# Gate projection tiles beside stick breaking and attention: weights loaded earlier, blocks dealt over other places

## The chip, the cores and the metric

The kernel runs on one core of a Trainium2 chip. The metric is the device time in microseconds of one execution; lower is better. Engines in the text: PE is TensorE (matmuls), DVE is VectorE, ACT is ScalarE, SP is the queue that issues the DMAs.

## What is computed

Two blocks of two layers each on 512 tokens of width 1024, in fp32. The second block's layer, cut to what matters here:

```python
def _layer(x, ...):
    h = _rmsnorm(x, norm_g)
    p = _split_columns(h @ w_in)
    y_a = _dsa_attention(q_a, k_a, v_a, qi, ki, p['idx_w'])   # index scores choose the keys
    y_b = _fox_attention(...)
    y_c = _stick_breaking_attention(sb_q, sb_k, sb_v)
    y_d = _nsa_attention(...)
    y_e = _memory_attention(...)
    ys = jnp.stack([y_a * silu(dsa_z), ..., y_e * silu(mem_z)], axis=2)
    merge = jax.nn.sigmoid(p['merge'].reshape(B, S, 5, D_MODEL))
    merged = jnp.sum(merge * jnp.einsum('bsnc,ncd->bsnd', ys, w_branch), axis=2)
    return x + merged @ w_out

def stick_breaking(q, k, v):
    z = q @ k.T * scale
    log_keep = where(strict, log_sigmoid(-z), 0)
    later = cumsum(log_keep, reverse=True) - log_keep
    a = where(strict, exp(log_sigmoid(z) + later), 0)
    return a @ v

# index scores: relu(qi_h @ ki.T) for 4 heads, weighted by idx_w and summed, causal
```

`merge` is a projection of `h` onto 5 x 1024 columns, 40 tiles of 128 columns.

## The kernel before

**Precision and gate blocks.** A weight tile (1024 x 128) is split in two fp32r parts: ACT casts the high part (`extra_high`, L1224), DVE subtracts to get the low part (`extra_low`, L1249). A tile is 8 blocks of 128 input channels; `block_passes` (L224 to L226) runs three matmuls for each block: high x high, high x low, low x high, 512 columns each.

**Extra.** 24 of the 40 gate tiles of a layer (3 of the 5 branches for each of 8 output tiles) are not computed in merge but "beside" other phases, while PE would wait there. The class `Extra` holds how many tiles, and a list of named slots with a number of blocks each. On PE, `extra_products(..., name)` runs the next blocks of that slot; at a tile's first block it waits for `split` (the low part of that tile) and for `evacuated` (the single PSUM bank is free again). On ACT, `extra_evacuations(name)` evicts all tiles that end up to that slot, and `extra_highs(name)` casts the tile two further on. On DVE, `extra_lows(name)` writes its low part. `slots_of` computes from the list which tiles are done by which name. SP loads the raw weights (`extra_load`) and writes evicted tiles to DRAM (`g_spill`, L1187), from where merge reads them.

**Order of the phases in a layer of block 2.** `project2` (34 projection tiles and small work beside them), `stick_breaking` (with 5 gate tiles), `attention` (with 19 gate tiles), `merge`. Each phase is a block with its own semaphores that ends with a barrier over all engines.

**Stick breaking** (L2908). On PE: logits of head 0 (four matmuls j = 0 to 3, L2959, in banks 0, 1, 2 and part of 1), slot "lead", then for each head h: index products of query block h+1 (four index heads, L2948), slot ("first", h), logits of head h+1, cumulative sums of head h (L2975, L2978, banks 4 to 6), slot h, product with the values (L2986). ACT: both first casts, then for each head the evacuation of the logits (L3002, L3003), Exp and Ln (L3005, L3007) in `logarithm`; in the loop the evictions of gates, relu of the index products (L3015), `logarithm(h+1)`, casts, and the Exp that gives the weights (L3027). DVE: low parts, softplus (L3038, L3043, L3047), index scores (`weigh`), the subtraction of the sums (L3076, then `less`), softplus of the next head, then `extra_lows`, then the output (L3084). The slots are 8 for lead, 2 before the logits of heads 1 to 3, then 6, 6, 6 and 8: 40 blocks. Index products use three banks, so the fourth waits for the first relu. The loads of the first four gate tiles are issued at the start of the phase, into `x`, whose space the projections still use for other weights up to their 32nd tile.

**Attention** (L2697). 12 pairs of heads x 4 query blocks make 48 steps; the loop runs s = -2 to 50. In step s PE runs the transposes of step s-1, the logits of s+2 (L2746), slot ("early", s), the values of s-2 (L2776), slot s. DVE masks (L2851), normalises (L2870), and up to step 31 ranks the index scores (L2881, L2887). Each slot has 2 blocks for s >= 0, so 4 a step; 19 tiles are 152 blocks and end with step 37. After all spills have landed SP issues the first loads for merge (`load_merge`, L1179).

Of the kernel before, what the change touches and what calls it, by code (L numbers as in the profile page):

```python
# [13 lines left out]
F32 = mybir.dt.float32  # L14
# [3 lines left out]
ACT = mybir.ActivationFunctionType  # L18
# [1156 lines left out]


def load_merge(sp, core, n, slot_w, width, src):

    sp.dma_start(core.ring[:, n * slot_w:n * slot_w + width], src).then_inc(core.landed[2][n], 16)  # L1179
# [1106 lines left out]

def project2(nc, core, units, b, p, gain, tmp, u_high, u_low, loads, landed, last_gain=None):

# [28 lines left out]
    with phase(nc, *LANDED, "projected", "evacuated", "scaled", "rounded", "split", *NORM, *OPENING, "params", "x_normed", "x_spilled",  # L2317
# [14 lines left out]
        def _(sp):  # L2332
# [22 lines left out]
            for n in range(RING, count):  # L2355
# [27 lines left out]
                if n == 30:  # L2383
                    sp.wait_ge(sems["mv_mm"], 1)
                    sp.dma_start(w1, b["w1_dram"]).then_inc(sems["w1_landed"], 16)
            sp.wait_ge(sems["params"], 16 * len(loads))
            sp.wait_ge(sems["index_copied"], 16)
# [520 lines left out]
def stick_breaking(nc, core, b, p, e):  # L2908
# [12 lines left out]

    cum = [(4, 0), (5, 0), (6, 0), (6, 256)]
    rel, score = b["rel"], b["score"]
# [10 lines left out]
    with phase(nc, *EXTRA, "rel_mm", "rel_out", "weighted", "z_mm", "z_out", "logged", "soft", "cum_mm", "less", "weights", "pv_mm", "y_out", "own", "own_act") as (block, sems):  # L2934
# [5 lines left out]
        def _(pe):  # L2940
            def index_products(i):

                for h in range(4):
                    if h < 3:
                        pe.wait_ge(sems["z_out"], 4 * (i - 1) + (1, 4, 3)[h])
                    else:
                        pe.wait_ge(sems["rel_out"], 4 * (i - 1) + 1)
                    pe.matmul(banks[h % 3][:, 0:(i + 1) * P], qi[32 * h:32 * h + 32, i * P:(i + 1) * P],  # L2948
                              ki[32 * h:32 * h + 32, 0:(i + 1) * P], start=True, stop=True).then_inc(sems["rel_mm"], 1)

            def logits(h):
                m, lo = h // 2, 64 * (h % 2)
                q, k = p[lo:lo + 64, tl["sb_q"] + m, :], p[lo:lo + 64, tl["sb_k"] + m, :]
                for j in range(4):
                    if h and j < 3:
                        pe.wait_ge(sems["rel_out"], 4 * (h - 1) + (4, 2, 3)[j])
                    if j == 3:
                        pe.wait_ge(sems["z_out"], 4 * h + 2)
                    pe.matmul(z_bank(j), k[:, j * P:(j + 1) * P], q[:, j * P:], start=True, stop=True)\  # L2959
                        .then_inc(sems["z_mm"], 1)  # L2960
# [3 lines left out]
            for h in range(4):  # L2964
                m, lo = h // 2, 64 * (h % 2)
                if h < 3:
                    index_products(h + 1)
                    extra_products(pe, sems, core, e, ("first", h))
                    logits(h + 1)
                pe.wait_ge(sems["soft"], h + 1)  # L2970
                if h:
# [19 lines left out]
        def _(act):  # L2991
# [5 lines left out]
            def logarithm(h):  # L2997
                if h >= 2:
                    act.wait_ge(sems["pv_mm"], h - 1)
                for j in range(4):  # L3000
                    act.wait_ge(sems["z_mm"], 4 * h + j + 1)
                    own(act.mul(span(zs, h, j), z_bank(j), SCALE))  # L3002
                    own(act.activation(span(soft, h, j), z_bank(j), ACT.Abs, scale=SCALE))  # L3003
                    own.tell(sems["z_out"])
                own(act.activation(whole(soft, h), whole(soft, h), ACT.Exp, scale=-1.0))  # L3005
                own.settle()
                act.activation(whole(soft, h), whole(soft, h), ACT.Ln, bias=core.ones[:, 0:1]).then_inc(sems["logged"], 1)  # L3007

            def relu(i):
                for h in range(4):  # L3010
                    n = 4 * (i - 1) + h
                    act.wait_ge(sems["rel_mm"], n + 1)
                    if i > 1:
                        act.wait_ge(sems["weighted"], n - 3)
                    act.activation(rel[:, h, 0:(i + 1) * P], banks[h % 3][:, 0:(i + 1) * P], ACT.Relu).then_inc(sems["rel_out"], 1)  # L3015

            extra_high(act, sems, core, e, 0)
            extra_high(act, sems, core, e, 1)
            logarithm(0)
# [11 lines left out]
        def _(dve):  # L3031
# [33 lines left out]

            own(dve.tensor_copy(score(0), causal(0)))
            extra_low(dve, sems, core, e, 0)
            extra_low(dve, sems, core, e, 1)
            softplus(0)
            for h in range(4):  # L3070
# [8 lines left out]
                if h < 3:  # L3079
# [5 lines left out]
                                  ALU.mult).then_inc(sems["y_out"], 1)  # L3085
            dve.wait_ge(sems["y_out"], 4)


# [15 lines left out]
def block2_layer(nc, core, layer, w, con, tables):  # L3104

    with ExitStack() as outer:
# [18 lines left out]
        b["f_abs"], b["f_log"] = buf(inner, "f_abs", [4, 4]), buf(inner, "f_log", [4, 4])  # L3125
        with split_weights(nc, core), nc.sbuf_tensor(f"norm_tmp3{layer}", [P, 4, T], F32) as tmp:
            loads = ((core.small[:, 0:NSMALL2], w["small2"][layer]), (tables[:, :, :], core.t_spill))
            if layer == 0:
                loads += ((con[:, :], w["con2"]),)
            project2(nc, core, lambda n: w["in2"][layer * IN2_TILES + n], b, p,  # L3130
                     core.par[:, PAR2["norm"]:PAR2["norm"] + KD] if layer else core.both_gains[:, :], tmp, u_high, u_low,
                     loads, core.landed[0], None if layer else core.gains[:, 0:KD])

# [3 lines left out]
        def stored_gate(t):  # L3137
            return gates(t // N_STORED * N_BR2 + N_BR2 - N_STORED + t % N_STORED)

        x_flat = core.x[:, :, :].rearrange("p a t -> p (a t)")  # L3140
        beside_stick = 5
        with ExitStack() as stack:
            b["cum"], b["stats"] = buf(stack, "cum", [2, T]), buf(stack, "stats", [3, 6])
            with ExitStack() as scratch:
# [13 lines left out]
                with nc.sbuf_tensor(f"rel{layer}", [P, 4, T], F32) as b["rel"], nc.sbuf_tensor(f"stick_low{layer}", [P, 2, KD * P], F32R) as core.wl:  # L3158
                    stick_breaking(nc, core, b, p, Extra(
                        stored_gate, 0, beside_stick, [("lead", 8), *((slot, n) for h in range(4) for slot, n in ((("first", h), 2 if h < 3 else 0),  # L3160
                                                                                                  (h, 6 if h < 3 else 8)))],
                        core.banks[3:4], [p[:, tl[n], :] for n in ("ckv", "kc_vc")]))
                core.wl = extra_low
# [40 lines left out]
                for m in range(2):  # L3204
                    pairs.append(pair("dsa", m, b["dsa_k"][:, m, :], head(b["dsa_v"], m), lambda h, i: b["score"](i)))
                attention(nc, core, b, pairs, forgotten, Extra(
                    stored_gate, beside_stick, KD * N_STORED - beside_stick,
                    [(slot, 2 if n >= 0 else 0) for n in range(-2, 4 * len(pairs) + 3) for slot in (("early", n), n)],
                    core.banks[7:8], [core.ring[:, n * T:(n + 1) * T] for n in range(2)]), gates)
# [56 lines left out]
def program(nc, w, positions, out):  # L3266
# [6 lines left out]
    with ExitStack() as stack:  # L3273
# [5 lines left out]
        core.count = 0  # L3279
        core.landed = [[stack.enter_context(nc.semaphore(f"{side}_{name}")) for name in LANDED] for side in ("one", "other", "third")]  # L3280
        core.last_spill = stack.enter_context(nc.semaphore("last_spill"))
        core.early = [stack.enter_context(nc.semaphore(f"early_gate{n}")) for n in range(2)]
# [84 lines left out]
```

## Time and profile before

| | us |
|---|---|
| median of 3 runs | 3474.04 (3471.01 to 3476.75) |
| profiled execution, its own time | 3477.62 |
| its span, first to last instruction | 3475.8 |
| granted TensorE clock, mean | 0.978 |

In the rows below, times are microseconds from the span's start. A row of the timeline has the start, the duration, engine, line, operation, output<-input, shapes and count; in brackets the idle time before it and what ended it. PEld is the weight load, which overlaps PE. A busy PE is not PE at its peak, since ends of matmuls are modelled.

### The profile page before, as it was taken

The page shows a single profiled execution, that of the slowest core. Times are in us where ns is not written, and L with a number is a line of the kernel's source. Part 1 is how long each engine was busy: PE and PEld are TensorE (multiplying, and loading weights), DVE is VectorE, ACT ScalarE, POOL GpSimd, SP SyncE. Part 2 cuts the span into 40 slices and gives each one's busy share as a digit, 9 for nine tenths or more (in the row PEclk, how much of TensorE's full clock was granted, in tenths as well). Part 3 has the DMA queues.
Part 4 walks back from the last instruction along what each step waited for, and adds up shares of the span by engine and source line. Part 5 has one row for each costly group of instructions (what it writes and reads, how often), then busy time and mean ns, then how long its engine had stood idle before and what let it go on. Part 6 is the DMA issues. An engine that isn't in the chain of part 4 may idle for free. (4 is left out here: it accounts for less than half of the span.)

```text
span 3475.8 us, 53876 instructions
## 1 busy us (share of the span) xinstructions
PE 3336.0 (96%) x21860; PEld 2610.6 (75%) x21860; DVE 1894.1 (54%) x3265; ACT 1434.2 (41%) x2357; POOL 58.5 (2%) x44
## 2 busy tenths in 40 slices
PE   8998999999999998999999999899899999999898
PEld 6776688788877876887888778566587787566686
DVE  6645634677556446446774452367555631476555
ACT  6423523444255224334443333545533343555532
POOL 0110000000000100000000000000000000000000
PEclk9999999999999999999999999899999999999999
DMA  4324232223232232422223252122152432121341
GB/s 157 95 67 169 97 107 81 103 97 104 100 124 94 76 98 111 155 100 85 97 93 110 102 173 97 40 83 82 35 191 94 152 117 104 47 78 58 127 140 67
DMA packets 106533, 356.86 MB, mean 103 GB/s; under 512 B 12544, under 2 KB 12928, under 8 KB 103488
## 3 DMA queue, kind: packets, MB, share of 16 engines
q1 hardware_dynamic: 106304, 353.67, 30.0%
q8 instruction: 160, 2.62, 0.3%
q14 instruction: 69, 0.57, 0.1%
HBM read 308.93 MB, written 38.80 MB: 100 GB/s over the span
## 5 line engine op out<-in xcount | busy, mean ns | idle before, releaser
L224 PE MATMUL banks<-h_high,weights_high 128*128 128x512 f32 x2464 | 993.8, 403 | 40.6 <-DVE weights_low L245 22.0
L225 PE MATMUL banks<-h_low,weights_high 128*128 128x512 f32 x2464 | 969.9, 394 | 0.0
L226 PE MATMUL banks<-h_high,weights_low 128*128 128x512 f32 x2464 | 969.1, 393 | 0.0
L224 PEld LDWEIGHTS banks<-h_high,weights_high 128*128 128x128 f32 x2464 | 466.8, 189 | 154.0 <-DVE weights_low L245 22.9
L226 PEld LDWEIGHTS banks<-h_high,weights_low 128*128 128x128 f32 x2464 | 466.6, 189 | 102.5
L225 PEld LDWEIGHTS banks<-h_low,weights_high 128*128 128x128 f32 x2464 | 467.3, 190 | 97.6 <-issue 3.3
L217 DVE TENSOR_TENSOR weights_low<-ring,weights_high 128x1024 fp32r<-128x1024 f32 x134 | 167.2, 1247 | 301.4 <-ACT weights_high L212 300.6
L1673 ACT CAST weights_high<-ring 128x1024 fp32r<-128x1024 f32 (+2 forms) x124 | 140.7, 1134 | 457.4 <-PE banks L226 457.2
L1721 DVE TENSOR_TENSOR weights_low<-ring,weights_high 128x1024 fp32r<-128x1024 f32 (+2 forms) x124 | 164.6, 1328 | 294.1 <-ACT weights_high L1673 293.9
L212 ACT CAST weights_high<-ring 128x1024 fp32r<-128x1024 f32 x134 | 140.4, 1048 | 363.9 <-PE banks L226 358.1
L1849 ACT CAST weights_high<-ring 128x1024 fp32r<-128x1024 f32 (+1 forms) x116 | 132.6, 1143 | 334.3 <-PE banks L226 334.3
L1896 DVE TENSOR_TENSOR weights_low<-ring,weights_high 128x1024 fp32r<-128x1024 f32 (+1 forms) x116 | 154.9, 1336 | 93.6 <-ACT weights_high L1849 93.3
L224 PE MATMUL banks<-h_high,extra_high 128*128 128x512 f32 x384 | 169.2, 441 | 1.2 <-ACT ring L1234 1.2
L225 PE MATMUL banks<-h_low,extra_high 128*128 128x512 f32 x384 | 152.7, 398 | 0.0
L224 PE MATMUL banks<-y_high,weights_high 128*128 128x512 f32 x352 | 136.9, 389 | 0.0
L225 PE MATMUL banks<-y_low,weights_high 128*128 128x512 f32 x352 | 136.9, 389 | 0.0
L226 PE MATMUL banks<-y_high,weights_low 128*128 128x512 f32 x352 | 136.9, 389 | 0.0
L224 PE MATMUL banks<-ffn_high,weights_high 128*128 128x512 f32 x352 | 136.9, 389 | 0.0
L225 PE MATMUL banks<-ffn_low,weights_high 128*128 128x512 f32 x352 | 136.9, 389 | 0.0
L226 PE MATMUL banks<-ffn_high,weights_low 128*128 128x512 f32 x352 | 136.9, 389 | 0.0
L226 PE MATMUL banks<-h_high,extra_low 128*128 128x512 f32 x304 | 120.4, 396 | 0.0
L224 PEld LDWEIGHTS banks<-h_high,extra_high 128*128 128x128 f32 x384 | 72.8, 190 | 47.2 <-issue 36.2
(454 smaller groups left out, 5049.5 us busy)
## 6 DMA issues: line engine op xcount, KB each, us to landing
ring<-in_in SPq DMA_DIRECT2D x136, 512.0 KB, 3.8
ring<-in_up SPq DMA_DIRECT2D x88, 512.0 KB, 3.2
ring<-in_gates SPq DMA_DIRECT2D x68, 512.0 KB, 3.6
x<-in_gates SPq DMA_DIRECT2D x60, 512.0 KB, 4.0
ring<-in_down SPq DMA_DIRECT2D x32, 704.0 KB, 4.1
ring<-in_out SPq DMA_DIRECT2D x32, 512.0 KB, 3.3
ring<-in_branch SPq DMA_DIRECT2D x16, 768.0 KB, 4.4
stored<-g_spill SPq DMA_DIRECT2D x16, 768.0 KB, 4.5
```

The costliest lines, as they stand in the source:

```text
L212: act.copy(core.wh[:, half, 0:width], slot(core, s[0], s[1])[:, 0:width]).then_inc(sems["rounded"], 1)
L217: dve.tensor_tensor(core.wl[:, half, 0:width], slot(core, s[0], s[1])[:, 0:width], core.wh[:, half, 0:width].bitcast(F32), ALU.subtract).t ...
L224: pe.matmul(bank, core.wh[:, half, w], high, start=start, stop=False)
L225: pe.matmul(bank, core.wh[:, half, w], low, start=False, stop=False)
L226: return pe.matmul(bank, core.wl[:, half, w], high, start=False, stop=stop)
L1673: act.copy(core.wh[:, n % 2, 0:width(n)], place(n)).then_inc(sems["rounded"], 1)
L1721: dve.tensor_tensor(core.wl[:, n % 2, 0:width(n)], place(n), core.wh[:, n % 2, 0:width(n)].bitcast(F32), ALU.subtract).then_inc(sems["spli ...
L1849: act.copy(core.wh[:, n % 2, 0:width(n)], place(n)).then_inc(sems["rounded"], 1)
L1896: dve.tensor_tensor(core.wl[:, n % 2, 0:width(n)], place(n), core.wh[:, n % 2, 0:width(n)].bitcast(F32), ALU.subtract).then_inc(sems["spli ...
```

## The change

In stick breaking there are now 6 gate tiles and in attention 18. The first two tiles' weights are loaded by SP in `project2` (at its tile 30, behind the load of `w1`) into columns 4096 to 6144 of the ring, each with its own semaphore; ACT waits for that instead of a load of its own phase. Two gate blocks are put into head 0's logits before the fourth matmul, and 3, 3 and 2 into those of heads 1 to 3 at the same place, in place of 2 each ahead of the logits. The slots after the sums have 7, 7, 8, 8 blocks. ACT casts the second tile after head 0's logits have been evacuated, not before. The fourth index product gets a bank of its own (6, shared with the sums); index products wait for all evacuated logits of the head before and for `less`; logits j waits for the relu of its own bank; the sums wait for all four relus. DVE copies the first score row after the first two low parts have been written. In attention the slots have 2 and 2 blocks up to step 15, 2 and 1 up to step 31, 1 and 1 after that.

```diff
+def early_stick(core, t):
+    return core.ring[:, (RING + t) * KD * P:(RING + t + 1) * KD * P]
...
@@ project2, SP
                 if n == 30:
                     sp.wait_ge(sems["mv_mm"], 1)
                     sp.dma_start(w1, b["w1_dram"]).then_inc(sems["w1_landed"], 16)
+                    for t in range(2):
+                        sp.dma_start(early_stick(core, t), first_gates(t)).then_inc(core.early_stick[t], 16)
...
@@ stick_breaking
-    cum = [(4, 0), (5, 0), (6, 0), (6, 256)]
+    cum, rel_banks = [(4, 0), (5, 0), (6, 0), (6, 256)], (0, 1, 2, 6)
...
             def index_products(i):
+                pe.wait_ge(sems["z_out"], 4 * i)
+                if i > 1:
+                    pe.wait_ge(sems["less"], i - 1)
                 for h in range(4):
-                    if h < 3:
-                        pe.wait_ge(sems["z_out"], 4 * (i - 1) + (1, 4, 3)[h])
-                    else:
-                        pe.wait_ge(sems["rel_out"], 4 * (i - 1) + 1)
-                    pe.matmul(banks[h % 3][:, 0:(i + 1) * P], ...)
+                    pe.matmul(banks[rel_banks[h]][:, 0:(i + 1) * P], ...)
...
                 for j in range(4):
                     if h and j < 3:
-                        pe.wait_ge(sems["rel_out"], 4 * (h - 1) + (4, 2, 3)[j])
+                        pe.wait_ge(sems["rel_out"], 4 * (h - 1) + j + 1)
                     if j == 3:
+                        extra_products(pe, sems, core, e, ("first", h - 1))
                         pe.wait_ge(sems["z_out"], 4 * h + 2)
...
                 if h < 3:
                     index_products(h + 1)
-                    extra_products(pe, sems, core, e, ("first", h))
                     logits(h + 1)
+                    pe.wait_ge(sems["rel_out"], 4 * (h + 1))
                 pe.wait_ge(sems["soft"], h + 1)
...
@@ stick_breaking, ACT
                     own.tell(sems["z_out"])
+                if h == 0:
+                    extra_high(act, sems, core, e, 1)
                 own(act.activation(whole(soft, h), whole(soft, h), ACT.Exp, scale=-1.0))
...
             extra_high(act, sems, core, e, 0)
-            extra_high(act, sems, core, e, 1)
             logarithm(0)
...
@@ stick_breaking, DVE
-            own(dve.tensor_copy(score(0), causal(0)))
             extra_low(dve, sems, core, e, 0)
             extra_low(dve, sems, core, e, 1)
+            own.settle()
+            dve.wait_ge(sems["split"], 2)
+            own(dve.tensor_copy(score(0), causal(0)))
             softplus(0)
...
+def beside_attention(steps):
+    slots = []
+    for s in range(-2, steps + 3):
+        early, late = (0, 0) if s < 0 else (2, 2) if s < 16 else (2, 1) if s < 32 else (1, 1)
+        slots += [(("early", s), early), (s, late)]
+    return slots
...
@@ block2_layer
-        beside_stick = 5
+        beside_stick = 6
...
-                        stored_gate, 0, beside_stick, [("lead", 8), *((slot, n) for h in range(4) for slot, n in ((("first", h), 2 if h < 3 else 0),
-                                                                                                  (h, 6 if h < 3 else 8)))],
-                        core.banks[3:4], [p[:, tl[n], :] for n in ("ckv", "kc_vc")]))
+                        stored_gate, 0, beside_stick, [(("first", -1), 2), ("lead", 8), *((slot, n) for h in range(4) for slot, n in (
+                            (("first", h), (3, 3, 2, 0)[h]), (h, (7, 7, 8, 8)[h])))],
+                        core.banks[3:4], [p[:, tl[n], :] for n in ("ckv", "kc_vc")],
+                        [(early_stick(core, t), core.early_stick[t], 16 * (layer + 1)) for t in range(2)]))
...
-                    [(slot, 2 if n >= 0 else 0) for n in range(-2, 4 * len(pairs) + 3) for slot in (("early", n), n)],
+                    beside_attention(4 * len(pairs)),
```

## Rows read from the trace of the kernel before

**Rows 1.** The page's first part: busy time, share of the span, instructions.

```profile
PE 3336.0 (96%) x21860; PEld 2610.6 (75%) x21860; DVE 1894.1 (54%) x3265; ACT 1434.2 (41%) x2357; POOL 58.5 (2%) x44
```

**Rows 2.** Busy time by stretch; stretch, its length, busy by engine, clock, DMA.

```profile
core 0: us, PE busy (x) PEld busy (x) DVE busy (x) ACT busy (x) POOL busy (x), PEclk, DMA share, GB/s
2190.90:2282.90 92.00, 78.96 (x288) 49.67 (x288) 37.42 (x77) 52.27 (x75) 0.00 (x0) 0.89 0.12 43
2282.90:2481.80 198.90, 197.53 (x1140) 135.70 (x1141) 136.01 (x508) 107.13 (x309) 0.00 (x0) 1.00 0.24 75
2361.00:2442.60 81.60, 81.39 (x486) 56.02 (x484) 58.87 (x209) 43.20 (x121) 0.00 (x0) 1.00 0.23 72
2481.80:2515.50 33.70, 24.48 (x197) 15.81 (x195) 16.29 (x75) 22.46 (x69) 0.00 (x0) 0.90 0.11 40
2938.10:3031.10 93.00, 78.76 (x288) 49.72 (x289) 37.42 (x77) 52.31 (x75) 0.00 (x0) 0.89 0.12 43
```

**Rows 3.** PE's waits in layer 0's stick breaking: total, times, longest.

```profile
PE banks L2959 <- ACTq L143: 8.8, 4, 5.3
PE banks L2948 <- ACT rel L3015: 1.7, 3, 0.7
PE banks L2986 <- ACT ring L3027: 1.0, 1, 1.0
```

**Rows 4.** Timeline of the start of layer 0's stick breaking, ACT.

```profile
2194.28 1.04 ACT L1224 CAST extra_high<-x 128x1024 fp32r<-128x1024 f32 x1 [4.15 <-DMA x<-in_gates]
...
2196.58 0.59 ACT L3002 ACTIVATE ring<-banks 128x512 f32<-128x512 f32 x1
...
2203.99 1.37 ACT L3007 ACTIVATE ring<-ring,ones 128x1280 f32<-128x1280 f32 x1
```

**Rows 5.** Timeline from the end of head 0's cumulative sums.

```profile
2218.28 0.48 PE L224 MATMUL banks<-h_high,extra_high 128*128 128x512 f32 x1
...
2218.56 1.68 DVE L3076 SCALAR_TENSOR_TENSOR ring<-banks,ring 128x512 f32<-128x512 f32 x4 [7.08 <-PE banks L2975]
...
2220.39 1.49 DVE L3038 SCALAR_TENSOR_TENSOR ring<-ring 128x1280 f32<-128x1280 f32 x1
...
2221.92 0.90 DVE L3043 TENSOR_TENSOR ring<-ring,con_sb 128x128 f32<-128x128 f32 x4
...
2223.52 0.57 ACT L1234 COPY others<-banks 128x512 f32<-128x512 f32 x1
...
2223.90 1.22 DVE L1249 TENSOR_TENSOR stick_low<-x,extra_high 128x1024 fp32r<-128x1024 f32 x1
```

**Rows 6.** Timeline, PE: the first passes of two gate blocks in succession.

```profile
2203.20 0.39 PE L224 MATMUL banks<-h_high,extra_high 128*128 128x512 f32 x1
...
2203.90 0.39 PE L224 MATMUL banks<-h_high,extra_high 128*128 128x512 f32 x1
```

**Rows 7.** Timeline near the end of the projections: issues on SP, a cast.

```profile
2147.55 7.88 SPq L2357 DMA_DIRECT2D ring<-in_in  x3
...
2163.98 1.05 ACT L212 CAST weights_high<-ring 128x1024 fp32r<-128x1024 f32 x1 [3.11 <-PE banks L226]
```

**Rows 8.** Busy time by stretch, columns as in rows 2: clock 0.50.

```profile
2198.50:2202.60 4.10, 3.86 (x9) 2.98 (x10) 0.00 (x0) 3.72 (x7) 0.00 (x0) 0.50 0.20 80
...
2254.10:2260.90 6.80, 6.70 (x13) 4.05 (x14) 0.00 (x0) 6.37 (x10) 0.00 (x0) 0.50 0.00 0
...
2510.10:2513.50 3.40, 3.40 (x21) 2.73 (x19) 0.00 (x0) 1.44 (x4) 0.00 (x0) 0.50 0.02 5
```

**Rows 9.** PE's waits in attention's steps 38 to 50: total, times, longest.

```profile
PE banks L2762 <- DVE probs L2870: 7.9, 3, 3.5
```

**Rows 10.** Timeline: last spill, merge's loads, its first cast; then their landing.

```profile
2482.65 0.32 SPq L1187 DMA_DIRECT2D g_spill<-ring  x1
...
2484.68 0.81 SPq L1179 DMA_DIRECT2D ring<-in_gates  x2
...
2517.11 0.40 ACT L235 CAST weights_high<-ring 128x256 fp32r<-128x256 f32 x1 [2.74 <-PEq L167]
...
DMA to landing us min/median/max: 3.6/4.1/4.6
```

More of the change, by code:

```diff
@@ L2284, with project2 @@
 TURN_AT = (5, 6, 7, 8, 9, 10, 11, 12, 15, 16)
-def project2(nc, core, units, b, p, gain, tmp, u_high, u_low, loads, landed, last_gain=None):
+def project2(nc, core, units, b, p, gain, tmp, u_high, u_low, loads, landed, first_gates, last_gain=None):
     con, small, par, banks, tables = b["con"], core.small, core.par, core.banks, b["tables"]
@@ L2941, in index_products @@
             def index_products(i):
+                pe.wait_ge(sems["z_out"], 4 * i)
+                if i > 1:
+                    pe.wait_ge(sems["less"], i - 1)
                 for h in range(4):
-                    if h < 3:
-                        pe.wait_ge(sems["z_out"], 4 * (i - 1) + (1, 4, 3)[h])
-                    else:
-                        pe.wait_ge(sems["rel_out"], 4 * (i - 1) + 1)
-                    pe.matmul(banks[h % 3][:, 0:(i + 1) * P], qi[32 * h:32 * h + 32, i * P:(i + 1) * P],
+                    pe.matmul(banks[rel_banks[h]][:, 0:(i + 1) * P], qi[32 * h:32 * h + 32, i * P:(i + 1) * P],
                               ki[32 * h:32 * h + 32, 0:(i + 1) * P], start=True, stop=True).then_inc(sems["rel_mm"], 1)
@@ L3014, in relu @@
                         act.wait_ge(sems["weighted"], n - 3)
-                    act.activation(rel[:, h, 0:(i + 1) * P], banks[h % 3][:, 0:(i + 1) * P], ACT.Relu).then_inc(sems["rel_out"], 1)
+                    act.activation(rel[:, h, 0:(i + 1) * P], banks[rel_banks[h]][:, 0:(i + 1) * P], ACT.Relu).then_inc(sems["rel_out"], 1)
             extra_high(act, sems, core, e, 0)
-            extra_high(act, sems, core, e, 1)
             logarithm(0)
@@ L3125, in block2_layer, with gates, stored_gate @@
         b["f_abs"], b["f_log"] = buf(inner, "f_abs", [4, 4]), buf(inner, "f_log", [4, 4])
+        def gates(n):
+            return w["gates2"][layer * (KD * N_BR2) + n]
+        def stored_gate(t):
+            return gates(t // N_STORED * N_BR2 + N_BR2 - N_STORED + t % N_STORED)
         with split_weights(nc, core), nc.sbuf_tensor(f"norm_tmp3{layer}", [P, 4, T], F32) as tmp:
@@ L3131, in block2_layer @@
                      core.par[:, PAR2["norm"]:PAR2["norm"] + KD] if layer else core.both_gains[:, :], tmp, u_high, u_low,
-                     loads, core.landed[0], None if layer else core.gains[:, 0:KD])
-        def gates(n):
-            return w["gates2"][layer * (KD * N_BR2) + n]
-        def stored_gate(t):
-            return gates(t // N_STORED * N_BR2 + N_BR2 - N_STORED + t % N_STORED)
+                     loads, core.landed[0], stored_gate, None if layer else core.gains[:, 0:KD])
         x_flat = core.x[:, :, :].rearrange("p a t -> p (a t)")
-        beside_stick = 5
+        beside_stick = 6
         with ExitStack() as stack:
@@ L3280, in program @@
         core.landed = [[stack.enter_context(nc.semaphore(f"{side}_{name}")) for name in LANDED] for side in ("one", "other", "third")]
+        core.early_stick = [stack.enter_context(nc.semaphore(f"early_stick{n}")) for n in range(2)]
         core.last_spill = stack.enter_context(nc.semaphore("last_spill"))
```

## The prediction

> **What bounds the kernel now.** I read the page's busy line first: the tensor engine (PE) is busy 96% of the span, VectorE (DVE) 54%, ScalarE (ACT) 41% [rows 1]. So time can be won only where PE stands still or runs at its lower clock, and lost wherever a change makes it wait. Second, the busy time by stretch [rows 2]: stick breaking takes 92.0 us in layer 0 and 93.0 in layer 1, both at a granted clock of 0.89; attention's steps 0 to 37 take 198.9 us with PE full; its steps 38 to 50, which carry no gate blocks, take 33.7 us with only 24.48 busy at clock 0.90. Those are the two stretches that the change touches, once per layer. Third, PE's waits in stick breaking [rows 3]: 8.8 us for the evacuated logits (5.3 of it at the start), 1.7 for the fourth index product, 1.0 for the weights. Fourth, the start in order of time [rows 4]: ACT idles until the first gate weights land, casts them at 2194.28 and 2195.62, and only then evacuates the logits. Fifth, head 0 from its index products to the next head's [rows 5]; this chain carries the forecast.
>
> A gate block is three passes; blocks follow each other every 0.70 us at clock 1.00 [rows 6], and I take twice that at 0.50.
>
> **Where the gate tiles now begin.** Gate tiles are 8 blocks. The first block of tile t waits for `split` t+1 (DVE's low part of tile t) and for tile t-1 to be evicted, since there is one bank. ACT and DVE do both at fixed places of their programs, which the diff leaves: ACT evicts at the start of each head's turn (`extra_evacuations`), DVE writes the low part after the next head's softplus (`extra_lows`). Before, tiles 0 to 4 end with the lead, slot 0, slot 1, slot 2 and slot 3, so each low part has been written, and each bank emptied, by the next tile's start. After, the order is 2 (inside head 0's logits), 8 (lead), 3, 7, 3, 7, 2, 8, 8. Tile 1 begins with block 8, two blocks before the lead's end; tile 2 with block 16, after 3 blocks of slot 0; tile 3 with block 24, after 1 block of slot 1; tile 4 with the first block of slot 2; tile 5 with the first of slot 3. PE is in order: the values product, the next index products and the next logits stand behind the waiting block.
>
> **Price of these waits.** From the end of the cumulative sums (first gate of slot 0, 2218.28) DVE subtracts from 2218.56 (1.68 us), then softplus 1.49, 0.90, 0.90, and the low part from 2223.90 to 2225.12 [rows 5]: 6.84 us after the slot began. The subtraction hangs on those sums and the rest stands behind it in DVE's program, so none of it comes sooner. Less what PE still has of the old tile: slot 0 6.84 - 3 x 0.70 = 4.7 us, slot 1 6.1, slot 2 6.8. In slot 3 there is no softplus: 0.28 + 1.68 + about 0.1 + 1.22 = 3.3. Sum 20.9. ACT's eviction comes sooner, 5.2 us after the slot's begin plus its cast (2218.28 to 2223.52) [rows 5], so DVE decides. In the lead, ACT needs from its first logits evacuation to the end of the second logarithm 2196.58 to 2205.36, 8.8 us [rows 4]; it can now start about 1.2 us into the phase, loses 1.5 waiting for the last logits behind two slow gate blocks, and casts tile 1 (1.04) in between; with the eviction (0.6) that is about 13.3 us; PE, done with tile 0 at about 9.9, waits 3.4 (0 to 4).
>
> **What it removes.** The loads under the start: 5.3 us (the first logits' last product then follows two gate blocks, at the lower clock, at about 5.2 us instead of 7.8). The three later waits for the logits, 3.5, are covered by 2 or 3 blocks (1.4 to 2.1 us against 1.2 each). The wait for weights 1.0 goes, as PE comes later. The fourth index product no longer waits, but the first logits product now waits for the first relu, which is the same event; of 1.7 I take 0.7 as won. Sum 10.5. The moved gate tile adds 8 x 0.70 = 5.6. The two extra loads queue on SP before tile 31's, which had 16 us in hand (issued 2147.55, cast 2163.98) [rows 7]; two more loads of 512 KB, each under 4 us to landing by the start of [rows 4] (phase begin 2190.9, cast 2194.28), don't use that up, so nothing. The moved copy of the first score (0.23 us of idle DVE) and the wait before it: nothing, DVE then waits for the logarithm anyway. The added waits, for all four relus before the sums and for `less` before the index products: ACT and DVE passed both earlier (the values product waited for the weights, which need `less`), nothing.
>
> **The clock.** In layer 0's stick breaking PE works at a granted clock of 0.50 in three stretches, the first 2198.5:2202.6 and the last 2254.1:2260.9 [rows 8], with 3.4 us between them: 14.3 us with PE nearly full, some 7 us lost; each follows a PE wait (5.3, 1.2, 1.2) [rows 3]. After there are five waits of 3.3 to 6.8 us. After the 5.3 us wait PE worked 4 us at half speed, which is 2 us lost; five of that kind, less for the short ones, is 8 us, against 7 before: +1 (bounds -5, all recover at once, to +8, each like 2254.1:2260.9 with 3.4 us lost). The Trainium skill (TensorE: Matmul & The Clock Gate, HAM oscillation — how this bites in real kernels) charges a long wait of the matmuls twice, once idle and once in slow work behind it; the stretch behind the 5.3 us wait agrees, clock 0.50 for 4.1 us. By that page alone, which speaks of long waits, the short waits of before would have cost no clock and the change would pay some 6 us more a layer; by the rows they cost most of the 7 us, and the measured rows decide.
>
> Stick breaking per layer: 20.9 + 3.4 - 10.5 + 5.6 + 1 = **+20.4 us**; the lead's and first blocks' pieces overlap a little, I take +19.5 (14 to 25).
>
> **Attention.** Before, 19 tiles at 4 blocks a step fill steps 0 to 37. After, 18 tiles: 4 in steps 0 to 15, 3 in 16 to 31, 2 in 32 to 47. Steps 16 to 37 lose 16 + 12 = 28 blocks, 19.6 us of a full PE. Steps 38 to 47 gain 20, 14.0 us. The tail's own work is 24.48 less half of two stretches of 3.4 us at 0.50 (the second in [rows 8]), 21.1; its waits (7.9 us for DVE's probabilities) [rows 9] are hidden by 1.4 us of gates a step, but for some 1.5. A new end: the last tile ends with step 47. Its eviction (0.6 + 0.1), the spill to its landing (2482.65 to 2484.68, 2.03) and then the load for merge (3.6 to 4.6 to landing, plus issue) [rows 10] make 6.5 to 7.5 us to merge's first cast, with 3.1 us of PE work under it: 3.9. Before, that load had been there for 30 us and merge cast at 2517.11 [rows 10]. So from 2481.8 to the cast: 21.1 + 14.0 + 1.5 + 3.9 = 40.5 against 35.3, +5.2. In steps 16 to 31 PE had 81.60 us and DVE 58.87 busy [rows 2]; with 11.2 us less of gates and two lows fewer DVE is at about 80%, near enough that some narrow steps wait (each also ranks, about 1.5 us). Two tiles end inside an early slot and wait for their eviction, which I put at 1 to 2 us each (0.59 for it and ACT's place in its step). I take 3 us (0 to 7). Sum -19.6 + 5.2 + 3 = **-11.4** (-15 to -7).
>
> **Sum.** Per layer 19.5 - 11.4 = +8.1, twice +16.2. The profiled execution took 3477.62 us (span 3475.8), so 3493.8; the median of the three runs is 3474.04, 3.6 lower, hence **3490.2 us**, 0.47% slower.
>
> **Rivals.** (A) *The boundary waits don't bite* (I misplace a boundary, or the low parts come in time): 5.6 - 10.5 and about 5 us of clock back, -9.9 a layer, with attention -11.4: -42.6, 3431. For it: before, all slots start without such a wait [rows 3]; against it: the block counts above and the DVE chain of [rows 5]. It decides if the first block of slot 2 starts within 1 us of the sums' end. Chance 0.08. (B) *The two halves cancel*: stick breaking at its low end (+14, clock recovers at once), attention at its best (-14): 3474, within 7 us. For it: both bounds are real. Chance 0.15. (C) *The clock and DVE make it worse*: every wait is followed by a long cold stretch, +25, and steps 16 to 31 become DVE's, -7: +36, 3510. For it: the 6.8 us stretch behind a wait of 1.2 us; against it: only 4.1 us of slow work behind the longest wait [rows 8]. Chance 0.12. The forecast, 3481 to 3503: 0.63; a mild form of A, 3450 to 3467: 0.02.
>
> **Range and chances.** 3472 to 3509 leaves out A in both forms, a third of B and the far part of C. A difference of 0.2% (7 us) is about what can be told from none. Faster 0.10, same 0.15, slower 0.75.
>
> **What would show it.** In the changed trace: PE waiting for DVE's `stick_low` before a gate block four times a layer, 4.7, 6.1, 6.8, 3.3 us, and for ACT's eviction once, about 3.4; `L2959` no longer waiting 5.3; stick breaking about 111 us; PE near full in steps 38 to 47, steps 16 to 31 at about 70 us plus waits, and merge's first cast waiting for its load. Wrong if the gate blocks of slots 1 and 2 run without a wait, or if attention shrinks by under 7 us.

## The result, and the profile after

The changed kernel takes 3509.75 us, the median of 3509.64 to 3519.69. The kernel before, on the same chip, takes 3473.95 (3471.01 to 3476.75). The ratio is 1.0107, with an interval of 1.0092 to 1.0121. The forecast was 3490.2: slower, as it turned out, but by 16 us where 35.8 were measured, and 0.75 us beyond the end of the range. The profiled execution has a span of 3507.8 us, 32.0 more than before's 3475.8.

The page's busy line of the changed kernel, answering to [rows 1]. PE is busy 9 us longer for the same 21860 instructions, while DVE and ACT have not changed: the rest of the 32 us, about 23, is PE standing still.

```profile
PE 3345.4 (95%) x21860; PEld 2611.6 (74%) x21860; DVE 1893.1 (54%) x3265; ACT 1432.9 (41%) x2357; POOL 58.5 (2%) x44
```

Busy time by stretch of the changed kernel, columns as in [rows 2]: stick breaking of layers 0 and 1, then attention of layer 0 from step 16 on, in two parts (steps 16 to 31, and step 32 to merge's first cast). After them, the same two parts in the kernel before. A step is cut at its logits, so 48 and 32 gate blocks lie in the two parts after, 64 and 24 before.

```profile
2190.30:2301.60 111.30, 84.58 (x313) 55.20 (x313) 38.70 (x78) 53.07 (x77) 0.00 (x0) 0.89 0.09 33
2951.10:3069.80 118.70, 91.48 (x313) 59.18 (x313) 38.70 (x78) 53.11 (x77) 0.00 (x0) 0.83 0.08 32
2386.00:2463.80 77.80, 74.59 (x463) 49.58 (x461) 58.27 (x212) 45.13 (x125) 0.00 (x0) 1.00 0.18 55
2463.80:2528.40 64.60, 58.53 (x397) 37.29 (x396) 31.11 (x131) 38.75 (x118) 0.00 (x0) 1.00 0.10 35
```

```profile
2367.40:2452.60 85.20, 84.99 (x509) 58.83 (x508) 61.85 (x219) 47.87 (x130) 0.00 (x0) 1.00 0.20 63
2452.60:2517.10 64.50, 53.70 (x374) 35.99 (x372) 29.04 (x122) 37.68 (x115) 0.00 (x0) 0.95 0.09 34
```

With the phases cut at the first logits, at attention's first forget products and at merge's first cast, the 32.0 us divide like this (us, layer 0 / layer 1):

| | before | after | difference | forecast |
|---|---|---|---|---|
| stick breaking | 92.1 / 93.0 | 111.3 / 118.7 | +19.2 / +25.7 | +19.5 each |
| attention to merge's first cast | 234.1 / 236.4 | 226.8 / 228.3 | -7.4 / -8.1 | -11.4 each |
| merge to the next stick breaking / to the end | 421.1 / 208.3 | 422.7 / 209.7 | +1.6 / +1.4 | 0 |

The projections ahead of them give back 0.6; that leaves 0.2 to rounding.

PE's waits in layer 0's stick breaking (total, times, longest; [rows 3] before), and below the fence's "..." the same in layer 1:

```profile
PE banks L224 <- DVE stick_low L1254: 20.3, 4, 6.7
PE banks L224 <- ACT queries L1239: 3.1, 1, 3.1
PE banks L2966 <- ACT rel L3024: 1.7, 3, 0.7
...
PE banks L224 <- DVE stick_low L1254: 20.8, 5, 6.6
PE banks L224 <- ACT queries L1239: 3.1, 1, 3.1
```

The waits for `stick_low` and for the eviction (`queries`, L1239) are new, and all of [rows 3] but the relu's wait are gone. One by one in the timeline of PE (start, duration, the wait ahead of the row in brackets), the first block of tiles 1 to 5:

```profile
2203.50 0.47 PE L224 MATMUL banks<-h_high,extra_high 128*128 128x512 f32 x1 [3.14 <-ACT queries L1239]
...
2222.31 0.50 PE L224 MATMUL banks<-h_high,extra_high 128*128 128x512 f32 x1 [4.56 <-DVE stick_low L1254]
...
2246.71 0.79 PE L224 MATMUL banks<-h_high,extra_high 128*128 128x512 f32 x1 [5.94 <-DVE stick_low L1254]
...
2272.08 0.80 PE L224 MATMUL banks<-h_high,extra_high 128*128 128x512 f32 x1 [6.65 <-DVE stick_low L1254]
...
2290.28 0.50 PE L224 MATMUL banks<-h_high,extra_high 128*128 128x512 f32 x1 [3.15 <-DVE stick_low L1254]
```

The forecast had 3.4, 4.7, 6.1, 6.8 and 3.3. What PE does behind them differs. A pass inside a group lasts 0.39 at full clock [rows 6]; behind the first row here, in the lead, the passes last 0.39, behind the other four most last 0.63 and follow each other every 0.43 us in place of 0.23. So behind four of the five waits of layer 0 the granted clock is 0.50, for 3.4, 6.8, 6.8 and 3.4 us, part of the middle two still within the wait. In layer 1 the lead's wait is followed by slow work too, the longest of all. The 13.7 us that begin 1.1 us ahead of that first row, in layer 0 and in layer 1:

```profile
2202.38:2216.08 13.70, 12.12 (x54) 8.08 (x55) 5.89 (x15) 9.57 (x18) 0.00 (x0) 1.00 0.05 19
2963.30:2977.00 13.70, 12.13 (x29) 6.97 (x29) 5.52 (x14) 4.80 (x12) 0.00 (x0) 0.50 0.05 20
```

PE is as busy in both and gets 29 matmuls done in place of 54. The chain behind the wait in slot 0, the counterpart of [rows 5]:

```profile
2215.70 1.68 DVE L3086 SCALAR_TENSOR_TENSOR ring<-banks,ring 128x512 f32<-128x512 f32 x4 [6.70 <-PE banks L2982]
...
2221.03 1.23 DVE L1254 TENSOR_TENSOR stick_low<-x,extra_high 128x1024 fp32r<-128x1024 f32 x1
```

The low part ends at 2222.26, and the block that needs it starts at 2222.31.

### The profile page after: what moved, and what is told of

Same layout as the page of the kernel before. It is cut to its first block and busy times, and to the rows that moved or that the text cites. A ratio compares the mean times of both kernels' runs of the same rounds, so it can differ in the third digit from the quotient of the medians.

```text
span 3507.8 us, 53884 instructions
## 1 busy us (share of the span) xinstructions
PE 3345.4 (95%) x21860; PEld 2611.6 (74%) x21860; DVE 1893.1 (54%) x3265; ACT 1432.9 (41%) x2357; POOL 58.5 (2%) x44
## 5 line engine op out<-in xcount | busy, mean ns | idle before, releaser
L224 PE MATMUL banks<-h_high,extra_high 128*128 128x512 f32 x384 | 182.3, 475 | 54.5 <-DVE stick_low L1254 41.1
L2810 ACT ACTIVATE probs<-probs,stats 128x128 f32<-128x128 f32 (+4 forms) x192 | 96.9, 507 | 69.3 <-DVE stats L2862 69.3
```

Source lines behind the costliest of these rows:

```text
L224: pe.matmul(bank, core.wh[:, half, w], high, start=start, stop=False)
L2810: act.activation(l, l, ACT.Exp, scale=SCALE, bias=stats[:, s % 3, 2 + h:3 + h], accum_out=stats[:, s % 3, 4 + h:5 + h]).then_inc(sems["exp ...
```

## The experiments

Each ran beside the kernel before on the same chip; "before" is the median of those runs. In the diffs, "-" is the changed kernel's line unless another is named.

**One half at a time.** *e1* takes the changed kernel with attention's old dealing, four blocks a step:

```diff
-        early, late = (0, 0) if s < 0 else (2, 2) if s < 16 else (2, 1) if s < 32 else (1, 1)
+        early, late = (0, 0) if s < 0 else (2, 2)
```

> The changed kernel with attention's 18 gate tiles dealt as before (4 blocks a step, ending with step 35). Theory 1 (the loss is in stick breaking): its two phases keep the 19.3 and 25.7 us that the trace of the changed kernel shows against before, and attention is shorter by the moved tile alone, 5.6 us a layer: 3474 + 45 - 11 = about 3508 us, the same as the changed kernel within 5 us. Theory 2 (the new dealing in attention costs much of the 36 us): this kernel falls to 3495 or below.

Measured: 3523.17 us against 3473.89, ratio 1.0134 (1.0111 to 1.0158). Stick breaking took 118.1 and 114.8 us at clock 0.83 and 0.87. So the loss sits in stick breaking, and the rival falls. It was 15 us more than the theory said. One of its four executions took 3510.37 and the others 3522 to 3525, as three of the changed kernel's took 3509.7 and one 3519.69; the clock is the first suspect, since the changed kernel's own two layers, with the same stick-breaking program, took 111.3 and 118.7.

*e2* takes the kernel before with the new dealing alone (19 tiles, so the middle stretch ends at step 34):

```diff
-[(slot, 2 if n >= 0 else 0) for n in range(-2, 4 * len(pairs) + 3) for slot in (("early", n), n)],
+beside_attention(4 * len(pairs)),     # (2, 2) to step 15, (2, 1) to 33, (1, 1) to 47
```

> The kernel before with its 19 tiles of attention dealt over all steps (4 blocks to step 15, 3 to step 33, 2 after). By the trace of the changed kernel attention gained 7.4 to 8.1 us a layer, 5.6 of it the moved tile, and merge started 1.5 us worse: 3474 - 2 x 2 + 3 = about 3473 us, no change. By the prediction's own term (-11.4 with 5.6 for the tile) it would be 3474 - 12 = 3462 us.

Measured: 3478.43 against 3473.89, 1.0018 (1.0006 to 1.0030); attention took 235.1 and 236.5 us where before took 234.1 and 236.4. The dealing by itself brings nothing; the profiled execution (3473.99) is one of the fastest of its ten, 4.4 us below their median. PE's waits in it, layer 0:

```profile
PE banks L224 <- ACT ring L1234: 3.6, 7, 1.2
PE banks L2762 <- DVE probs L2870: 2.6, 2, 1.6
...
PE banks L224 <- DVE weights_low L245: 7.0, 1, 7.0
```

The waits for DVE's probabilities fell from 7.9 [rows 9] to 2.6, and those for ACT's copies of the turned probabilities from 1.3 to none: 6.6 won. Evictions of tiles that end in the middle of a step rose from 0.6 to 3.6, and merge's first product waits 7.0 where it waited 2.5: 7.5 lost. Net +0.9, measured +1.0 in layer 0 (+0.1 in layer 1). Its stick breaking, which the edit leaves alone, took 89.3 and 89.8 us here, and 90.4 and 93.2 in e5 below, against 92.1 and 93.0: what an unchanged stage can differ by.

**Tiles that end with their slots.** *e3* takes the changed kernel with five tiles of eight blocks, dealt so that each ends with the lead or a slot; everything else of the change in stick breaking stays, and attention deals its 19 tiles as in e2:

```diff
-        beside_stick = 6
+        beside_stick = 5
-                        stored_gate, 0, beside_stick, [(("first", -1), 2), ("lead", 8), *((slot, n) for h in range(4) for slot, n in (
-                            (("first", h), (3, 3, 2, 0)[h]), (h, (7, 7, 8, 8)[h])))],
+                        stored_gate, 0, beside_stick, [(("first", -1), 2), ("lead", 6), *((slot, n) for h in range(4) for slot, n in (
+                            (("first", h), (3, 3, 2, 0)[h]), (h, (5, 5, 6, 8)[h])))],
```

> The changed kernel with 5 gate tiles in stick breaking, dealt 2, 6, 3, 5, 3, 5, 2, 6, 8, so that each tile ends with a slot again; attention as in e2_attention_alone. All else of the change stays: early loads, gates between the logits, fourth bank. Theory 1 (the waits at tile boundaries are the loss): no wait for stick_low in the slots, stick breaking about 80 us a layer against 92 before, 3474 - 24 = about 3450 us. Theory 2 (the early loads, the gates between the logits or the new waits of the index products cost by themselves): stick breaking above 92 us, 3474 us or more.

Measured: 3455.24 against 3473.89, 0.9950 (0.9934 to 0.9967). Stick breaking by stretch, and PE's waits in it:

```profile
2189.80:2269.30 79.50, 72.41 (x288) 46.70 (x289) 37.41 (x77) 51.73 (x75) 0.00 (x0) 0.96 0.12 43
```

```profile
PE banks L2966 <- ACT rel L3024: 3.9, 3, 2.7
PE banks L2993 <- ACT ring L3035: 1.6, 2, 1.4
```

No gate block waits any more, and the stage is 12.6 us shorter than before and 31.8 shorter than in the changed kernel, 5.6 of that the sixth tile. So the place of the tile boundaries turned a gain into a loss. Part of the gain is clock: of the 12.6 us, 6.5 are PE's busy time for the same 288 recorded products.

*e4* takes the changed kernel with DVE's low part ahead of the next head's softplus; nothing else moves:

```diff
+                extra_lows(dve, sems, core, e, h - 1 if h else "lead")
                 if h < 3:
                     softplus(h + 1)
-                extra_lows(dve, sems, core, e, h - 1 if h else "lead")
```

> The changed kernel with DVE writing the low part ahead of the next head's softplus, not behind it. The low part is then ready about 3.3 us earlier, but the bank is evicted only about 5.3 us after the slot's begin. If both are needed: the waits of slots 0 to 2 fall from 4.6, 5.9, 6.7 to about 3.5, 3.8, 4.8 us and are put down to ACT's eviction; 5 us a layer and some clock, about 3498 us. If the low part alone decides: they fall by 3.3 us each, about 3488 us. If the wait is for something else: 3510 us.

Measured: 3495.95 against 3473.89, 1.0071 (1.0054 to 1.0087): 13.8 less than the changed kernel. PE's waits in layer 0's stick breaking:

```profile
PE banks L224 <- ACT others L1239: 7.5, 2, 4.2
PE banks L224 <- ACT queries L1239: 6.6, 2, 3.4
PE banks L224 <- DVE stick_low L1254: 3.1, 1, 3.1
```

DVE's wait is replaced, in three slots out of four, by a shorter one for ACT's eviction, which stands at a fixed place of ACT's program. In slot 3, where no softplus stood ahead, the wait for DVE stays at 3.1. This is what the forecast's chain says, since it had the eviction next in line. The profiled execution (3490.47) is the fastest of the four.

**The other half repaired.** *e6* and *e7* are e3 with other dealings in attention: the old one, and one in which every tile ends with a slot and the next begins a step later.

```diff
-        early, late = (0, 0) if s < 0 else (2, 2) if s < 16 else (2, 1) if s < 34 else (1, 1)   # e3
+        early, late = (0, 0) if s < 0 else (2, 2)                                               # e6
+        early, late = (0, 0) if s < 0 else (2, 2) if s < 20 else ((2, 1), (2, 1), (2, 0))[(s - 20) % 3]   # e7
```

> e3_tiles_end_with_slots with attention's 19 tiles dealt as before, 4 a step. If the dealing over all steps loses by itself, as e2_attention_alone has it (4.5 us slower than before): 3455 - 4.5 = about 3450 us. If it gains once stick breaking is mended: 3460 us or more.

> e3_tiles_end_with_slots with attention's tiles ending at the ends of steps too: 4 blocks to step 19, then 3, 3 and 2 in turn, so the last tile ends with step 46. Theory (eviction waits inside slots, 3.0 us more a layer than before, and merge's first load behind the last spill, 2 to 4.5 us a layer): both go, about 3455 - 11 = 3444 us. If group changes cost more than both: within 3 us of 3455.

Measured: e6 3452.34 and e7 3441.46, both against 3474.37; ratios 0.9935 (0.9918 to 0.9951) and 0.9901 (0.9885 to 0.9918). Attention took 234.2 and 236.0 us in e6, 228.8 and 227.5 in e7. PE's waits in e7's attention, layer 0:

```profile
PE banks L224 <- DVE weights_low L245: 2.5, 1, 2.5
PE banks L2769 <- DVE probs L2877: 1.8, 1, 1.8
PE banks L2769 <- ACT ring L2822: 1.8, 4, 0.6
...
PE banks L224 <- ACT ring L1239: 0.6, 3, 0.2
```

The eviction waits are back at 0.6 and merge's first product at 2.5, while the tail's gain stays. e7 is the fastest version, 33 us under before.

*e12* is the same dealing in the kernel before, with the old stick breaking:

> The kernel before, stick breaking untouched, attention's 19 tiles dealt over steps 0 to 46 so that tiles end with steps (4, then 3, 3, 2 in turn). e2_attention_alone had 7 eviction waits (3.6 us) and merge's first load late (7.0 us before its first gate product); by e7 both shrink: 5.5 us a layer less than before, 3474 - 11 = about 3463 us. If the dealing over all steps brings nothing: 3474 us.

Measured: 3463.14 against 3474.61, 0.9963 (0.9951 to 0.9976), attention 227.5 and 229.0: the aligned dealing is worth 11 us with either stick breaking (e6 to e7: 10.9).

**A theory that fell.** In the timeline, PE stands still for a moment each time it changes between narrow products and gate blocks, and I supposed that fewer, longer groups of gate blocks would save these moments. *e5* (kernel before) and *e8* (e6) put all four blocks of a step into its early slot:

```diff
-[(slot, 2 if n >= 0 else 0) for n in range(-2, 4 * len(pairs) + 3) for slot in (("early", n), n)],                    # before
+[(slot, k if n >= 0 else 0) for n in range(-2, 4 * len(pairs) + 3) for slot, k in ((("early", n), 4), (n, 0))],       # e5
-        early, late = (0, 0) if s < 0 else (2, 2)                                               # e6
+        early, late = (0, 0) if s < 0 else (4, 0)                                               # e8
```

> The kernel before with attention's 4 gate blocks of a step in one place (all ahead of the values, none behind) and not 2 and 2. In e2_attention_alone a group of a single block takes 0.88 us (2489.82 to 2490.70) where a block inside a group takes 0.70, and PE idles 0.17 to 0.33 us ahead of many groups. Theory G (each change between gate blocks and attention's own matmuls costs about 0.25 us): 38 groups fewer a layer, 19 us less, about 3455 us. Rival (groups cost nothing, and the second place hides a wait for the evacuated probabilities): 3474 us or more.

> e6_ends_and_old_dealing with the 4 gate blocks of a step in one place. By theory G 19 us less than e6, about 3431 us; by its rival the same as e6, about 3450 us.

Measured: e5 3480.27 against 3474.37, 1.0009 (0.9999 to 1.0019); e8 3456.38 against 3474.37, 0.9947 (0.9930 to 0.9963), 4 us more than e6. The theory is off by its size and by what it left out; attention took 235.5 us in e5 against 234.1. The timelines give what a group costs beyond 0.70 us a block: from its first pass to the next other matmul a group of four takes 2.98 us, one of two 1.55 (means), a lone block 0.88 (median, changed kernel behind step 32), so 0.15 to 0.18 each. Making one group of two saves 2 x 1.55 - 2.98, 0.12 us a step, in 38 steps some 5 us a layer and not 9.5. Against that, PE works longer at clock 0.50 in e5's attention (17.1 us of layer 0 against 6.8, 3.5 us lost):

```profile
2281.10:2516.55 235.45, 223.11 (x1336) 153.62 (x1336) 152.28 (x582) 130.02 (x379) 0.00 (x0) 0.96 0.22 69
```

**The clock.** *e9* is the changed kernel in which PE, ahead of each boundary wait, runs matmuls whose results nobody reads (12 to 27 passes, as long as the wait); they are added work, and nothing of the kernel's own is left out.

```diff
         if k == 0:
+            fill = getattr(e, "fill", {}).get(t)      # {1: (4, 12), 2: (8, 18), 3: (12, 24), 4: (16, 27), 5: (16, 12)}
+            if fill:
+                pe.wait_ge(sems["z_out"], fill[0])
+                for r in range(fill[1]):
+                    pe.matmul(core.banks[0][:, :], core.hh[:, r % KD, 0:P], core.hh[:, r % KD, :], start=True, stop=True)
             pe.wait_ge(sems["split"], t + 1)
```

> The changed kernel with idle matmuls ahead of each of the five boundary waits (12, 18, 24, 27 and 12 passes of 0.23 us into a free bank, their results are dropped), a little shorter than the waits of 3.1, 4.6, 5.9, 6.7 and 3.2 us. The waits stay, PE is busy in them. If the lower clock behind the waits is what made stick breaking 118.7 us in layer 1 and 111.3 in layer 0: the clock stays near 1.00 there, both take about 102 us, 3509 - 25 = about 3485 us. If the clock hangs on something else, or the clock costs nothing: 3509 us.

Measured: 3491.14 against 3474.61, 1.0043 (1.0029 to 1.0057), which is 18.6 less than the changed kernel. Stick breaking of both layers by stretch:

```profile
2191.10:2295.50 104.40, 98.89 (x405) 67.17 (x406) 38.73 (x78) 53.15 (x77) 0.00 (x0) 0.98 0.10 36
2948.10:3053.05 104.95, 98.94 (x405) 67.35 (x406) 38.73 (x78) 53.16 (x77) 0.00 (x0) 0.98 0.10 36
```

The waits' time is still spent, now on filler (the longest remaining wait for the low part is 0.5 us, in layer 1 0.7), yet the stage is 6.9 us shorter in layer 0 and 13.7 in layer 1, and both layers take the same time within 0.6 us. That is the price of the lower clock behind the waits. It is not the whole price of the lower clock in the stage: 3.4 us at 0.50 near the stage's start stay.

**What the parts are worth.** *e10* is the kernel before with the early loads alone (and the first score row copied behind their low parts):

```diff
+                    for t in range(2):
+                        sp.dma_start(early_stick(core, t), first_gates(t)).then_inc(core.early_stick[t], 16)
```

*e11* is e7 with the three index banks of before and the waits that they need (shown is the bank table; the order of the waits goes back with it):

```diff
-    cum, rel_banks = [(4, 0), (5, 0), (6, 0), (6, 256)], (0, 1, 2, 6)
+    cum, rel_banks = [(4, 0), (5, 0), (6, 0), (6, 256)], (0, 1, 2, 0)
```

> The kernel before with the first two gate tiles' weights of stick breaking loaded by the projections (and the first score row copied after their low parts), nothing else. The wait of 5.3 us at the start falls to about 2 (both casts, 2.1 us, still stand ahead of the logits' evacuation): 3.4 us a layer and up to 2 us of clock, 3474 - 9 = about 3465 us. If the loads disturb the projections: 3474 us or more.

> e7_ends_in_both with the index products in three banks again, with their waits of before. The fourth product then waits for the first relu and the first logits for the last relu: about 1 us a head, 3 heads, 2 layers, 3441 + 6 = 3447 us. If the bank does nothing: 3441 us.

Measured, both against 3474.61: e10 3465.36, 0.9974 (0.9962 to 0.9986), stick breaking 85.8 and 85.7 us, 6.3 and 7.3 less than before, 3.7 of it shorter waits for the evacuated logits. e11 3453.89, 0.9934 (0.9918 to 0.9951), which is 12.4 more than e7. Stick breaking in e11, with the same columns:

```profile
2191.10:2279.80 88.70, 79.85 (x289) 49.94 (x289) 37.44 (x77) 52.14 (x75) 0.00 (x0) 0.90 0.10 39
```

PE's waits in that stretch are 3.9, 1.7 and 1.6 us, where e3 has 3.9 and 1.6; the 1.7 is what comes back. The rest is PE's busy time, 79.85 against 72.41 for the same products, and the clock, 0.90 against 0.96: the fourth bank and its waits pay mostly through the clock, 7.4 of 9.2 us. This holds beside the other parts of the change. With three banks and everything else of it, the stage takes 88.7 us, 2.9 more than with the early loads alone (e10), so putting gate blocks between the logits lost time without the fourth bank. The fourth bank in the kernel before was not run.

## Why the forecast was right in direction and short in size

**The boundary waits: right.** Each of the five was measured within 0.3 us of its forecast. The work without the clock was about right too: before's 92.0 us less the 7 that I gave to its clock is 85.0, and 20.9 + 3.4 - 10.5 + 5.6 more make 104.4; e9, where the clock stays up but for those 3.4 us (1.7 lost), takes 104.4 and 105.0. e3 and e4 confirm the cause, the place where a tile ends and what stands ahead of its low part.

**The clock: a mis-sized term, about 6 us of the miss.** The step that failed is "five of that kind, less for the short ones, is 8 us", one value for both layers. By e9 it is 6.9 in layer 0 and 13.7 in layer 1. The upper bound that I gave, each wait followed by a long stretch at 0.50 with 3.4 us lost, is near what layer 1 showed; I read one value from one wait (2 us lost behind the 5.3 us wait) and used it for five. Nor was that slow work the wait's alone: in the kernel before the clock is 0.50 from 2192.5 on, ahead of the wait, and the changed kernel, which has no wait there, is at 0.50 for 3.4 us at the same place. The waits of the two layers are equal (20.3 and 3.1 against 20.8 and 3.1), so they can't tell the layers apart; the granted clock does. At 0.83 of 118.7 us PE had the lower of its two clocks, 1.2 GHz, for about 40 us, at 0.89 of 111.3 for about 24 (twice the share missing to 1). Half of the 16 us between them is 8 us, against 7.4 measured. Most of it is the one stretch of 13.7 us behind the lead's wait shown above: a wait of 3.1 us, just as long in layer 0, that cost nothing there. e1 shows 118.1 and 114.8 for the same program; the long stretch is in its layer 0, and in its layer 1 the lead's wait is followed by 3.4 us at 0.50. So the same wait had three outcomes in four executions of the stage, and what picks one stays open.

**Attention: short by 4.0 and 3.3 us, in layer 0 nearly all of it after step 31.** Steps 16 to 31 went from 85.20 us to 77.80, -7.4: PE's busy time fell by 10.4 for 16 blocks less, and eviction waits of 3.1 came in place of 0.2. I had -11.2 and +3, read from the stretch 2361.00:2442.60 of [rows 2], which really begins ahead of step 15's logits and ends at step 30's; four tiles end in the middle of a step, not two, and no step waited for DVE's ranks. From step 32 to merge's first cast I had 12 blocks less (-8.4) and +5.2, together -3.2; measured was 64.50 to 64.60, +0.1. The recovered clock, for which I took 3.4 us off, came: 1.00 against 0.95, and no slow stretch is left. The failed step is the price of the blocks, 0.70 us each wherever they stand. Behind step 32 the eight blocks more (20 gained, 12 lost) should have raised PE's busy time by 5.6 less 3.4, 2.2 us; it rose by 4.8. The 24 blocks there of before stand in 12 groups of two, 1.55 us a group to the next other matmul, 18.6 us. The 32 of after stand alone, at 0.94 us in the mean, of which 0.08 is the wait for the probabilities behind some: 27.5 us, so 8.9 more and not 5.6; that is the size of what is missing. The first pass of such a group lasts longer than the one inside it:

```profile
L224 PE MATMUL banks<-h_high,extra_high 128*128 128x512 f32 x24 | 10.7, 446 | 0.0
...
L224 PE MATMUL banks<-h_high,extra_high 128*128 128x512 f32 x32 | 15.9, 498 | 0.0
```

(The first of these lines is before's, the second the changed kernel's; 446 and 498 are mean ns.) This is read from the two timelines; no run varies the groups behind step 32 alone, and layer 1 was not taken apart in this way. PE's idle time fell by 4.7 where I had 5.4. e2 has the same lone blocks, and there too the sum of its waits, +0.9, gives the measured +1.0 with nothing left over from the clock.

**Merge and the end: put at nothing, +3.0 us.** The stage after attention took 1.6 and 1.4 us longer. PE's busy time rose by just that, 1.6 and 1.4, for as many matmuls, at a granted clock of 0.98 against 0.99 and 0.95 against 0.96: it is the lower clock again. In layer 0 the one slow stretch more, 3.4 us, comes right behind PE's wait for merge's first weights, 4.4 us where before had 2.5. In e12, where that wait is 2.5 again, the stage takes 421.0 us as before. It took 1.9 to 5.0 us longer than before also in e1 to e5, e8 and e9, and about 1 in e6 and e7; in e4, where it is 5.0, PE's busy time rose by 4.9, and a second slow stretch, of 6.8 us, lies in the next layer's projections, far from any edit. Why the clock falls there is open.

**The sum.** Forecast +16.2, clock of layer 1 +6.2, layer 0 -0.3, attention +4.0 and +3.3, merge and end +3.0, -0.6 ahead of stick breaking: 31.8 of the 32.0. The medians differ by 3.8 more, since before's profiled execution lay 3.6 us above its median and I took that distance off the forecast; the changed kernel's did not lie above its own.

**The rivals.** A falls: all boundary waits bite. B falls by stick breaking alone. C's time, 3510, is the measured one, by luck in good part: its +25 for stick breaking came true in layer 1 (+25.7) but not in layer 0 (+19.2). Its reason for attention, steps 16 to 31 bound by DVE, did not show; the -7 came about as told above, and it has no term for merge. Of what was removed, the early loads alone gave 6.3 and 7.3 us in e10, where both casts still stand ahead of the evacuation; I had 5.3 for the wait and counted the clock apart.

## What to carry to other kernels

When work in tiles is dealt over the slots of another stage, count blocks to each tile boundary and look at what the boundary waits for; a boundary anywhere but at the end of a slot whose name the other engines work by costs the whole distance to the fixed place where they prepare the next tile (here two boundaries lay inside slots behind the sums, one in the lead, and two just ahead of such a slot, one of which cost the most, 6.7 us). Spreading the same blocks with boundaries at those ends turned +36 us into -33. Price each new wait of PE twice: its own length, and the slow work behind it, which here was between 30% and 60% of the waits' sum, and for a single wait of 3.1 us anything from nothing to 6 us. And price a block by the group it stands in, not by its pitch inside a long one.

## What the runs showed of the hardware

- The granted clock, not the waits, made two executions of one stage differ by 7.4 us (0.89 and 0.83), with waits equal to 0.5 us. A stretch of 13.7 us at 0.50, behind a wait that left the clock at 1.00 in the other layer, makes most of it. With PE kept busy through the waits, both layers agreed to 0.6 us at 0.98.
- Short waits cost clock as well. In e10 PE waits in layer 0's stick breaking for nothing longer than 1.6 us, and the clock is still only 0.92. Its largest group of waits there:

```profile
PE banks L2966 <- ACTq L143: 5.1, 4, 1.6
```

  The Trainium skill (TensorE: Matmul & The Clock Gate) charges long waits in its section "HAM oscillation — how this bites in real kernels", and in "A second HAM failure mode: psum-queue depth-cycling" it has short idle moments between groups of matmuls bring the clock down too. By the first section alone the clock of e10 would have been full; the trace speaks for the second. The prediction's "by that page alone" holds for the first section only.
- A fourth PSUM bank for products that rotated through three, with its waits, took 1.7 us of waiting away and raised the clock from 0.90 to 0.96: PE's busy time for the same 288 or 289 recorded products fell by 7.4 us (e11 against e3).
- A gate block of three 512-column passes takes 0.70 us inside a group, 0.78 in a group of two and 0.88 alone (median) between narrow products, all at clock 1.00.
